# A hybrid encoder layer: dot products moved between stages, and one reload issued ahead of weight units

## The reference

```
act = gelu(einsum('phkd,pd->phk', u[eidx], tok))     # u, v: 16384 rows of 1024 f32
out = einsum('phk,phkd->pd', softmax(best) * act, v[eidx])
```

## Time and profile before

| | us |
|---|---|
| median of 3 runs (lowest, highest) | 1890.25 (1888.90, 1890.81) |
| the profiled execution | 1892.49 |
| its span, first to last instruction | 1890.6 |

### The profile page before, as it was taken

One profiled execution on the slowest core, in us unless ns is written; L12 is line 12 of the kernel. 1 busy time (PEld: TensorE's weight loads), 2 busy tenths in 40 slices (PEclk: granted clock), 3 DMA queues, 4 the chain that ended last, 5 costly groups with the idle time before them and its releaser, 6 DMA issues.

```text
span 1890.6 us, 34413 instructions
## 1 busy us (share of the span) xinstructions
PE 1816.0 (96%) x12531; PEld 1203.5 (64%) x12542; DVE 1541.8 (82%) x2941; ACT 860.5 (46%) x1310; POOL 1061.8 (56%) x668
## 2 busy tenths in 40 slices
PE   9999999999998999999988999999799999999996
PEld 7647777777777856566655666666466655555554
DVE  7975656455356589999999989886899999999997
ACT  6445446565445545333334656655333333333331
POOL 2732222222234849688889887787556555555551
PEclk9999999999999999999999999999899999999998
DMA  5632114222454536799999999999999999999993
GB/s 207 213 117 93 57 46 117 99 88 88 138 179 157 190 105 218 225 330 321 307 325 379 382 410 410 405 413 376 352 406 408 406 408 406 407 406 404 399 366 122
DMA packets 164094, 514.47 MB, mean 272 GB/s; under 512 B 18616, under 2 KB 47296, under 8 KB 163464
## 3 DMA queue, kind: packets, MB, share of 16 engines
q1 hardware_dynamic: 57152, 204.54, 30.0%
q0 software_dynamic: 55296, 201.35, 28.1%
q10 hardware_dynamic: 51528, 107.04, 15.2%
HBM read 456.98 MB, written 55.88 MB: 271 GB/s over the span
## 4 chain that ended last, share of the span: by engine, by line
PE 46%; DVE 30%; DMA 13%; issue 5%; POOL 2%; ACT 2%; ACTq 1%; DVEq 0%; SPq 0%
PE ps L2005 22%; DMA rows<-in_v_units,rowi 11%; PE ps L2124 10%; DVE rows L1750 5%; DVE accS L1897 4%; PE ps L2021 3%; DVE w_lo L1880 3%; PE ps L2278 2%; DVE W_lo L1914 2%; POOL rows L674 1%; DVE wb L1931 1%; DVE eq L1736 1%; PE ps L2457 1%; PE ps L2458 1%; PE ps L2258 1%
## 5 line engine op out<-in xcount | busy, mean ns | idle before, releaser
L611 POOL TENSOR_TENSOR w_lo<-raw,w_hi 128x1024 bf16<-128x1024 f32 x250 | 544.2, 2184 | 477.7 <-ACT w_hi L739 442.9
L739 ACT ACTIVATE w_hi<-raw 128x1024 bf16<-128x1024 f32 x381 | 399.6, 1052 | 332.3 <-DMA raw<-in_v_units 100.2
L674 POOL DMA_INDIRECT rows<-in_v_units,rowi x192 | 285.5, 1487 | 231.4 <-DVE accS L1897 177.4
L2503 PE MATMUL ps<-W_hi,w_hi 128*128 128x384 bf16 x992 | 324.7, 327 | 22.1 <-DVE W_lo L1914 11.5
L2005 PE MATMUL ps<-h_hi,w_hi 128*128 128x384 bf16 x1024 | 335.7, 328 | 6.3 <-ACT hb L1138 6.2
L2005 PE MATMUL ps<-h_lo,w_hi 128*128 128x384 bf16 x1024 | 335.4, 328 | 0.0
L2005 PE MATMUL ps<-h_hi,w_lo 128*128 128x384 bf16 x1024 | 335.3, 327 | 0.0
L2503 PE MATMUL ps<-W_lo,w_hi 128*128 128x384 bf16 x992 | 324.4, 327 | 0.0
L2503 PE MATMUL ps<-W_hi,w_lo 128*128 128x384 bf16 x992 | 324.3, 327 | 0.0
L637 POOL DMA_INDIRECT rows<-in_u_rows,rowi x192 | 211.3, 1100 | 82.9 <-DVE dots L1750 35.3
L1750 DVE CUSTOM_DVE_ANT_0 rows<-rows,ps 128x1024 f32<-128x1024 f32 x192 | 227.5, 1210 | 8.5 <-DMA rows<-in_u_rows,rowi 7.9
(11 more groups left out here) (470 smaller groups left out, 3396.1 us busy)
## 6 DMA issues: line engine op xcount, KB each, us to landing
raw<-in_u_units SPq DMA_DIRECT2D x128, 512.0 KB, 6.1
raw<-in_v_units SPq DMA_DIRECT2D x128, 512.0 KB, 8.0
raw<-in_units SPq DMA_DIRECT2D x123, 512.0 KB, 3.4
hd<-hb ACTq DMA_DIRECT2D x120, 192.0 KB, 6.2
Hb<-hd ACTq DMA_DIRECT2D x30, 768.0 KB, 9.6
gd<-gsb ACTq DMA_DIRECT2D x48, 384.0 KB, 10.4
Gb<-gd ACTq DMA_DIRECT2D x14, 1152.0 KB, 23.3
gz<-stage ACTq DMA_DIRECT2D x24, 288.0 KB, 2.1
```

Source lines behind the costliest of these rows:

```text
L611: pool.tensor_tensor(w_lo[:, k % RING, :], raw[:, k % RAW, :], w_hi[:, k % RING, :], ALU.subtract).then_inc(lo_ready, 1)
L674: pool.indirect_dma_start(out=rows[:, row_slot(ND + n), :], out_offset=None, in_=table, in_offset=bass.IndirectOffsetOnAxis(ap=index, axis ...
L739: act.activation(w_hi[:, k % RING, :], raw[:, k % RAW, :], ACT.Copy).then_inc(hi_ready, 1)
L2503: ins = pe.matmul(ps[:, d, 0:TD], w[:, slot, d * P:(d + 1) * P], x[:, k, 0:TD], start=(first and w is w_hi and x is W_hi), stop=False)
```

## The change

The first `Gb` (the load at L564) is issued ahead of the first eight `v` units and not between the fourth and the fifth. 74 dots stand ahead of the gate steps and not 80 (six fewer in `DOTS_WAIT`), nine stand behind every four gate steps and not eight (108 in 48 steps and not 96: three behind every fourth), and 10 in the handover and not 16, with `gated(0)` behind the third, `gated(1)` and `w_low(0)` behind the seventh, and `w_low(1)` behind the last. The gathers' places follow from the same numbers.

```diff
-DOTS_EXP, DOTS_WAIT, DOTS_STEP = 8, 12, 2
+DOTS_EXP, DOTS_WAIT = 8, 6
+DOTS_FOUR = 9
...
 def dots_until(i):
-    return DOTS_BEFORE + DOTS_STEP * i
+    return DOTS_BEFORE + DOTS_FOUR * i // 4
...
     if s - RG < dots_until(N_STEP):
-        return J_G * BODY - 1 + (s - RG - DOTS_BEFORE) // DOTS_STEP * BODY // G_BODY
+        return J_G * BODY - 1 + (s - RG - DOTS_BEFORE) * 4 // DOTS_FOUR * BODY // G_BODY
...
-            for k in range(RAW):
-                load(a["v_units"][LAST_ON + k], (U_V + k) % RAW, False, U_V + k - RAW + 1)
             sp.wait_ge(paired, 1)
             for b in range(2):
                 sp.wait_ge(b_written[b], NBK // 2 * PIECES * 16)
             load_g(NCH // GG - 1, 0)
+            for k in range(RAW):
+                load(a["v_units"][LAST_ON + k], (U_V + k) % RAW, False, U_V + k - RAW + 1)
...
                 dot(s)
-                if s == dots_until(N_STEP) + 5:
+                if s == dots_until(N_STEP) + 2:
                     gated(0)
-                if s == dots_until(N_STEP) + 9:
+                if s == dots_until(N_STEP) + 6:
                     gated(1)
                     w_low(0)
-                if s == dots_until(N_STEP) + 13:
+                if s == ND - 1:
                     w_low(1)
```

## The result

| | before | changed |
|---|---|---|
| median, us (lowest to highest) | 1890.53 (1888.90 to 1899.13, 4 runs) | 1923.76 (1921.13 to 1927.89, 4 runs) |
| profiled execution, its span | 1892.49, 1890.6 | 1921.13, 1919.3 |
| gate step 0 starts; last product of the last gate step starts | 1014.9, 1303.4 | 1012.2, 1339.7 |
| V work of VectorE starts | 1348.94 | 1378.25 |

The change makes the kernel slower: ratio 1.0163, interval 1.0146 to 1.0181. The two spans differ by 28.7 us, and the marks of the table place it: the first step comes 2.7 us earlier, the way from it to the last one takes 39 us more (327.5 against 288.4), the handover 7.1 us less, and what follows the start of the V work as long as before (541.1 and 541.7). So the gate stage lost everything, and the term of the handover came as forecast.

A forecast was written before the change was run, and what follows sets the result against it. It took TensorE's chain to bound the gate stage, with DMA at a 416 GB/s ceiling, and TensorE, VectorE and DMA the V stage. Terms -6.5 + 6.5 - 7.1 = -7.1 us gave 1883 us, range 1873.5 to 1892.5.

The forecast's parts named there:

- the term of the handover: Handover: earlier Gb load and fewer dots let VectorE's V work start at G + 38.4, not G + 45.5: -7.1 us.
- The step that failed: Gate stage: 1.5 more dots per body cost VectorE 1.8 us, hidden by TensorE's work within 3.2 us of idle time.
- The cover that I named: Gate stage: three-dot steps fit because VectorE may run two steps, 9.6 us, ahead.
- Entry, -6.5: Ahead of the gate steps: with six fewer dots, step 4 comes at 1034.2 instead of 1040.69; bounds -3.1 and -11.2.
- the later low halves no longer bunch: Entry: six fewer gathers on POOL, 7.4 us, and 3.1 MB less DMA keep the later low halves apart.
- Gate stage, +6.5: Gate stage: added gathers bring 4.7 MB, 2.2 MB fit under 416 GB/s, the rest costs time; bounds 0 and +11.3.
- the slower one: Rival, gate stage: gelu waits for `hd` writes in ScalarE's two-buffer ring; 1 us longer landing gives +10.4, 1901; chance 0.10.
- the signs of being wrong: Gate slices of 425 GB/s or more, `gated(0)` waiting for a transfer, VectorE waiting for rows, or a longer V stage.
- signs of being right: Step 4 near 1034, gate stage some 6 us longer at 416 GB/s, TensorE waiting for gelu, V work at G + 38.

The follow-up runs named there:

- the fourth run: The changed kernel with every gather of the gate steps one unit later in POOL's list: 1889.4 us, ratio 0.9979.
- the eighth run: The changed kernel with gathers one unit later, but 17 dots in eight steps and 16 behind: 1891.72 us, ratio 0.9991.

## Why the prediction was wrong

**The step that failed** is "On VectorE 1.5 x 1.18 us [...] = 1.8 us, against 3.2 us of idle time, so TensorE's work hides it", which puts VectorE's part of the gate stage at nothing; measured are 39 us more between the first step and the last. The price per dot is right, 1.21 us as in the earlier trace rows. The 3.2 us per body were not room to spare, though, because the 201.2 us that I subtracted hold stretched instructions, and how many of them are stretched depends on when the work comes. Issued back to back, an undisturbed one-hot takes 0.60 us (1213.04 is followed by 0.68 us instructions 0.60 apart) and a dot with its accumulator read 1.14, so nine dots in four steps ask for 4 x 4 x 0.60 + 9 x 1.14 = 19.9 us, against TensorE's 36.7 x 4 / 6 = 24.5. If each set of one-hots meets one low half of 2.14 us, it is 28.4. The margin is there without the meetings and gone with them, and 12 times 28.4 is 341; measured were 327.5, since some steps are spared. Eight dots would ask for 18.7 us and with the meetings for 27.3, also more than 24.5. So the ninth dot doesn't decide by its price. What decides is whether the meetings are kept up, and they are where POOL waits for dots: 58.5 us in the changed kernel, 0.3 before, 2.4 with the gathers one unit later. The prediction had both halves in its own rows, 7.17 us beside three low halves, named them for the entry, and didn't ask what happens when the same pair meets in each of 48 steps.

**The cover that I named** for the three-dot steps ("VectorE may run two steps, 9.6 us, ahead") holds only while VectorE is faster. The rows that it needs are fetched by an engine that waits for its dots, and this return path stood in the code: `fetch` waits for dot s - 7. That the added gathers lie in POOL's idle time of 40.7 us counted busy time and not the wait in front of a gather, 58.5 us in 30 waits. What starts the beat, and why it holds at nine in four, no run here separates; the runs show that this rate is enough with either start (ratios 1.0163 and 1.0197), and that the early start with two dots per step is not.

**Entry, -6.5.** The run shows step 0 at 1012.20, 2.7 us before the 1014.94 at which the prediction held it, but step 4 at 1036.89 instead of 1034.2: 3.8 us gained. "So the later low halves no longer bunch" was wrong: four of them do, for 8.39 us. With the gathers one unit later step 4 comes at 1033.81, and there too four bunch, and a one-hot takes 7.61 us. So the size of the term was about right for a kernel without the beat, and its reason was not.

**Gate stage, +6.5.** Hidden in the changed kernel, which never gets to the bytes. With the gathers one unit later the six bodies run at 413 to 416 GB/s, and step 4 to G takes 271.9 us against 262.9: +9.0, within my bounds of 0 and +11.3. With the short low halves, where no one-hot of these steps is stretched, it is +9.3, so the one-hots are not what stretches the stage there. The two kernels with the low halves one step later that didn't lose lie above my bound, at +13.2 and +12.4. The Trainium skill, page "DMA: Bandwidth & Descriptors", section Specifications, gives 435 GB/s for the fabric; no body here passes 416 (single slices of 3 us reach 423), so the measurement decides for the lower figure for this mix. I can't call the ceiling shown as the only cause, since the smaller rate of the eighth run took as long, and the two kernels with two dots per step and one part of the change each are 2.3 and 2.7 us longer than before on this way without a byte more.

**Handover, -7.1.** Right in size and in its marks, in the changed kernel and in the fourth run's, whose V work also starts at G + 38.3. The move of the load alone brings 4.8 us of it in the profiled execution. The prediction's account of the handover before left out the same meeting: `gated(1)` took 7.30 us at 1330.84, beside three low halves from 1331.23, and takes 0.76 in the changed kernel. The V stage passes its start on, as forecast, to 1 us in these two kernels.

The fourth run's kernel, with the same dots, steps and loads, comes near the forecast but doesn't meet it. Its terms are -6.9, +9.0, -7.1 and, behind the start of the V work, -0.7 us, together -5.7 in the span (1884.9 against 1890.6) for a forecast of -7.1, and the profiled execution took 1886.76 for a forecast of 1885.4. Its median is 3.7 us below that of the kernel before, half of what was forecast.

**The rivals.** No rival has the result, 33 us slower; the slower one, with a chance of 0.10, was placed in ScalarE's ring and priced at +10.4. None of the signs of being wrong that the prediction lists came: the DMA didn't pass 425 GB/s, `gated(0)` waited for the gelu, VectorE didn't wait for rows, and the V stage was no longer. Of its signs of being right, TensorE was no longer busy all the time, but it waited for one-hots. The ring that closed was another one, that of the gathered rows, and the meetings of one-hots and low halves closed it. The Trainium skill, page "SBUF — State Buffer", section "Who interferes with whom", says that a VectorE instruction with two inputs in SBUF contends with a GpSimd instruction that reads SBUF, and that one of them then blocks for the whole of the other. The traces agree: the one-hots, with both inputs in SBUF, are stretched to 2.86 and 4.94 us, the dots, which read one operand from PSUM, never (the longest of 192 takes 1.22 to 1.24 us in every kernel here). From rows alone a rival could have been priced: 7.17 us beside three low halves is some 2.15 us for each, six sets per body are 12.9 us of VectorE's time, against 3.2 us of idle time.

## What to carry to other kernels

Idle time of an engine is no budget if part of its busy time is stretching: first take out what the stretched instructions take over their shortest, then ask what the sum is when every pair that can meet does. Wherever two engines wait for each other through a ring, a small delay can settle into a beat that costs the same at every turn; look for a new wait between just these two, and break it by moving one of them by half a turn. Move one thing only, since two cures in the same direction closed another loop here.

## What the runs showed of the hardware

A one-hot and a low half that meet don't share: one waits for the other and then does its own work. In the gate steps of the changed kernel it is the one-hot that waits (the low halves take 2122 to 2158 ns, 52 of them), also where its record starts first: 1213.04 and 1213.18, 1219.91 and 1220.07, 1185.49 and 1185.65. It isn't always so. In the kernel before, VectorE and then GpSimd:

```profile
1149.99 0.68 DVE L1869 TENSOR_TENSOR hot_lo<-hot,pair 128x1024 bf16<-128x1024 bf16 x1
```

```profile
1150.30 2.37 POOL L611 TENSOR_TENSOR w_lo<-raw,w_hi 128x1024 bf16<-128x1024 f32 x1
```

Here the low half waits, and ends 2.00 us behind the end of the one-hot. But with the same 0.31 us between the records, at 1154.72 and 1155.03, the one-hot waits and takes 3.02 us. So the order of the recorded starts doesn't tell who waits when they are this close. Between two low halves in a row the one-hot didn't get in at 1220.07; it ends 0.57 us behind the second. At the entry of the changed kernel it did: two low halves in a row at 1007.86 take 4.72 us, where those at 1220.07 take 4.21, and the second waits for a one-hot.

The best kernels here, with the gathers ahead of the wait (0.9968) or the low halves one step later (0.9972), beat both the one before and the changed one, though the one before by 0.3% only; their intervals overlap, and also overlap that of the later gathers (0.9979). Five placements of POOL's work with the same dots thus give medians of 1889.0, 1889.0, 1889.4, 1923.0 and 1923.8 us.
